# Sparse attention of the last mixers: two PSUM banks in turn in place of three

## The reference

```python
def one_block(args):                       # one block of 128 queries
    dots = jnp.einsum('bqhd,bsd->bqhs', iqb, ik) * idx_scale
    score = jnp.einsum('bqh,bqhs->bqs', iwb * w_scale, jax.nn.relu(dots))
    score = jnp.where(admissible[None], score.astype(jnp.float32), -jnp.inf)
    _, sel = lax.top_k(score, k_sel)       # 256 keys for each query
    ...
    logits = (jnp.einsum('bqhr,bqkr->bqhk', ql, c_sel).astype(jnp.float32) * scale
              + jnp.swapaxes(bias, -1, -2).astype(jnp.float32))
    p = jax.nn.softmax(logits, axis=-1).astype(c.dtype)
    return jnp.einsum('bqhk,bqkr->bqhr', p, c_sel)
```

## Time and profile before

| | before |
|---|---|
| median of three runs | 5201.58 us |
| lowest and highest | 5184.79 and 5215.15 us |
| span of the profiled execution | 5189.6 us |
| TensorE, VectorE, ScalarE busy in the span | 84%, 51%, 37% |
| the thirteen steps that attend tiles 15 to 3 | 3783 to 4945 us of the span |

### The profile page before, as it was taken

One profiled execution on the slowest core, in us unless ns is written; L12 is line 12 of the kernel. 1 busy time (PEld: TensorE's weight loads), 2 busy tenths in 40 slices (PEclk: granted clock), 3 DMA queues, 4 the chain that ended last, 5 costly groups with the idle time before them and its releaser, 6 DMA issues. The chain is left out here.

```text
span 5189.6 us, 65192 instructions
## 1 busy us (share of the span) xinstructions
PE 4361.9 (84%) x23554; PEld 3247.0 (63%) x23554; DVE 2639.9 (51%) x5371; ACT 1922.0 (37%) x3900; POOL 711.8 (14%) x745
## 2 busy tenths in 40 slices
PE   7997999984688888888898999977787878787679
PEld 6885777774566555656787888853344444454467
DVE  3113444445555544444212111138889888888545
ACT  3112323324323333333101101023667776777621
POOL 3102111100000000000000000003222333344400
PEclk9998999985567777778899999976677788778789
DMA  5327666664000000000423212120000000101033
GB/s 184 119 106 239 210 221 204 215 206 139 28 24 24 24 24 24 13 24 3 154 109 115 82 65 81 55 73 17 19 28 29 19 19 19 37 19 35 31 126 118
DMA packets 203393, 425.84 MB, mean 82 GB/s; under 512 B 37224, under 2 KB 67596, under 8 KB 202908
## 3 DMA queue, kind: packets, MB, share of 16 engines
q1 hardware_dynamic: 203072, 421.67, 23.7%
HBM read 299.93 MB, written 121.65 MB: 81 GB/s over the span
## 5 line engine op out<-in xcount | busy, mean ns | idle before, releaser
L3185 POOL TENSOR_TENSOR ds_E<-ds_bT 128x256 f32<-128x256 f32 x112 | 72.8, 650 | 2797.5 <-ACT ds_bT L3154 2620.6
L2718 PE MATMUL ds_big<-ds_ikT,ds_iqT 64*128 64x512 f32 (+3 forms) x608 | 382.0, 759 | 75.4 <-ACT ds_iqT L2695 54.6
L301 PE MATMUL g_acc<-g_ws_hi,g_hT_hi 128*128 128x512 f32 (+1 forms) x1024 | 386.5, 377 | 0.0
L303 PE MATMUL g_acc<-g_ws_hi,g_hT_lo 128*128 128x512 f32 (+1 forms) x1024 | 384.9, 376 | 0.0
L302 PE MATMUL g_acc<-g_ws_lo,g_hT_hi 128*128 128x512 f32 (+1 forms) x1024 | 384.9, 376 | 0.0
L529 PE MATMUL mm_big<-mm_gw_hi,mm_ghT_hi 128*128 128x512 f32 (+1 forms) x768 | 321.4, 418 | 31.0 <-PEq L134 31.0
L2774 DVE TENSOR_SCALAR_CACHE_REDUCE ds_seen<-ds_eq,ds_num 128x2048 uint16<-128x2048 uint16 (+13 forms) x224 | 331.3, 1479 | 26.4 <-issue 4.4
L531 PE MATMUL mm_big<-mm_gw_hi,mm_ghT_lo 128*128 128x512 f32 (+1 forms) x768 | 302.7, 394 | 0.0
L530 PE MATMUL mm_big<-mm_gw_lo,mm_ghT_hi 128*128 128x512 f32 (+1 forms) x768 | 302.0, 393 | 0.0
L2814 ACT ACTIVATE ds_signs<-ds_lo,ds_at 128x2048 bf16<-128x2048 uint16 (+13 forms) x224 | 291.3, 1301 | 1.5
L328 DVE COPY g_stage<-g_acc 128x512 f32<-128x512 f32 (+1 forms) x64 | 41.5, 649 | 459.2 <-PE g_acc L303 459.2
(11 more groups left out here) (519 smaller groups left out, 10155.1 us busy)
## 6 DMA issues: line engine op xcount, KB each, us to landing
mm_ghT_hi<-turned SPq DMA_DIRECT2D x96, 512.0 KB, 3.8
mm_ghT_lo<-turned SPq DMA_DIRECT2D x96, 512.0 KB, 5.5
proj<-g_stage SPq DMA_DIRECT2D x112, 256.0 KB, 2.0
proj<-mm_gstage SPq DMA_DIRECT2D x80, 256.0 KB, 5.0
mm_x<-proj SPq DMA_DIRECT2D x64, 256.0 KB, 3.8
second_raw<-in_w_in SPq DMA_DIRECT2D x56, 256.0 KB, 4.2
proj<-fp_stage SPq DMA_DIRECT2D x48, 256.0 KB, 2.0
mm_graw<-in_w_in SPq DMA_DIRECT2D x40, 256.0 KB, 6.4
```

The source lines that it names most:

```text
L301: pe.matmul(sums, hT.hi[:, k, tile], wt.hi[:, k, 0:width], start=(k == 0), stop=False)
L303: mm = pe.matmul(sums, hT.lo[:, k, tile], wt.hi[:, k, 0:width], start=False, stop=(k == KD - 1))
L2718: pe.matmul(big[:, n % 2, 0:wd], iqT[o, h // 2], b.ikT[o, x:x + wd], start=True, stop=True)\
```

## The change

The list of banks loses its last entry:

```diff
-    turns = in_turn([2, 3, 4], uses)
+    turns = in_turn([2, 3], uses)
```

## The result

| | before | after |
|---|---|---|
| median of four runs | 5204.64 us | 5252.98 us |
| lowest and highest | 5184.79 and 5215.15 us | 5248.38 and 5263.06 us |
| span of the profiled execution | 5189.6 us | 5248.3 us |
| steps that attend tiles 15 to 12 | 458.6 us | 498.8 us |

The kernel is 1.13% slower, ratio 1.0113 with a 95% interval of 1.0094 to 1.0133. Of 5204.64 us that would be 59 us; the two medians lie 48 us apart (0.93%), and the four runs of before scatter by 30 us. The profiled execution took 5250.26 us, of which 5248.3 are the span. So the loss is 48 to 59 us where 30 were forecast.

A forecast was written before the change was run, and what follows sets the result against it. The prediction took VectorE, which hardly ever waits, as the bound, with TensorE close behind. Terms of 20 + 9 + 6 less 5 us absorbed gave 30 us over the median, 5232 us, range 5196 to 5275.

The forecast's parts named there:

- By waits alone the change can only cost: Across the kernel: every old wait is implied by a new one, so nothing starts earlier unless a duration changes.
- term 3: TensorE's clock after longer holds: half of 7 holds at 3.4 us, half reaching VectorE, 6 us; upper bound 24.
- Term 1: L waiting for the previous piece's eviction: 1.0 us at 14 four-piece places, 0.3 at 20 others, 20 us; bounds 0, 53.
- both cases: Head 2 of tiles 14 and 15: the delayed L(2,1) makes L(2,2) late, costing VectorE 1.3 and 1.9 us.
- The worked case of tile 14: Head 2: L(2,1) starts 3.4 us later, work behind it moves 3.5 us, and VectorE loses 1.3 us at L(2,2).
- 34 places: Of some 127 L checked, those that started before the eviction would free one of two banks, 63.8 us together.
- Term 2: T waiting for ScalarE's previous copy in 43 places: 28 us on TensorE, a third counted, 9 us; bounds 0 and 28.
- Clock collapses: Four- and three-piece tiles: long holds send TensorE to 0.50, 24 to 32 episodes, 65 us, 5267 us; chance 0.11.
- if the clock of the steps moves by more than 0.04: Sign that the forecast is wrong, set on TensorE's clock in the steps attending tiles 15 to 3.
- Absorbed: TensorE's idle time in the thirteen steps makes good what is lost: 0 to 12 us, about 5208 us; chance 0.27.
- Every piece serialised: Heads 1 to 3: VectorE waits for each of 120 pieces' matmuls after evicting, 80 to 130 us, 5305 us; chance 0.07.
- Faster: Thirteen steps: TensorE works in denser stretches, its clock falls less often, 28 us less, 5174 us; chance 0.08.

The follow-up runs named there:

- idle holds: Kernel before, three banks; at seven places in tiles 15 to 12 L also waits, TensorE idle, for VectorE's eviction of the piece before: 5230.08 us, ratio 1.0062.
- busy hold: Kernel before, three banks; unread matmuls into L's own bank ahead of L(2,1) in tiles 15 to 12 and L(1,1) in 14 to 12: 5196.38 us, ratio 1.0016.
- e2_rest_only: Against the kernel before: three banks kept for the four-piece tiles, two for all others; 5204.33 us, ratio 1.0031.
- e6_l_later: Changed kernel with each L of heads 1 to 3 placed 0.45 of a piece later in TensorE's list; 5227.48 us, ratio 1.0067 to the kernel before.
- the two with idle holds: Kernel before with L waiting idle for the previous eviction: at seven places 5230.08 us, ratio 1.0062; at only the four L(2,1) 5217.71 us, ratio 1.0049.

## Why the prediction was right or wrong

- **Direction and place: right.** "By waits alone the change can only cost" held, VectorE is what a late logits matmul is lost on, and 40 us stand in the steps of tiles 15 to 12, as said. VectorE's wait for L grew to 62.1 us ("35 us or more"). But these steps grew by 9 to 13 us each, where 3 to 6 were forecast.
- **The step that failed: term 3, with the 6 us for the clock.** It took half of seven long holds to lower the clock, at 3.4 us of TensorE each, and half of that for VectorE. The busy and the idle holds, at seven places, differ in VectorE's wait by 43.7 - 13.1 = 30.6 us, of which 19.2 us are the waits for the four L(2,2). Three errors are in the term. First, the half: the seven were the four L(2,1), and L(3,1) of tiles 11, 9 and 7, and all four L(2,1) lowered the clock; by themselves they make 27.2 of the 34.0 us of the idle holds. Of the other three in the changed kernel the one in tile 7 did (3.85 us), those in tiles 11 and 9 (2.56 and 1.30 us) did not. Second, the price: the low clock comes when TensorE has the two score matmuls, the recurrence's group, a T, a `weigh` and the next L before it, so that 5.3 us of work become 10.2, 4.9 us and not 3.4. Third, halving for VectorE: it has at that place run out of work, and all 4.9 us arrived.
- **Term 1, 20 us for L behind the eviction: too large for what it described.** I worked both cases with full-clock durations. Such a delay without the clock, the busy hold, costs 3.4 us of VectorE's wait over seven of the dearest places, 0.5 us each, where I took 1.0; the whole time says 4 us by the medians and 8 by the ratio. The worked case of tile 14 came to 1.3 us; the busy hold leaves 0.41 us at L(2,1) and nothing at L(2,2). I also counted 34 places late against the eviction; 24 holds are there, 44.9 us, probably since VectorE's later evictions and TensorE's later L move together. The wait was forecast at 40 to 70 us in 35 places.
- **Term 2, 9 us for T behind the copy: small, as taken, and no more.** With two banks for L and one for T the kernel is at +0.12% (-0.01 to +0.24%), so 6 us with an interval from 0 to 12; the upper bound of 28 us is out. The waits moved from `weigh` to T as described.
- **Luck in the sum.** Terms 1 and 2 were put too high for the four-piece tiles and term 3 far too low. The errors offset each other in part, so that 30 us look nearer to the 48 to 59 measured than the mechanism was.
- **The rivals.** "Clock collapses" had the right cause and was given 0.11. It asked for a mean clock of 0.75 or less over the steps; over tiles 15 to 3 it went from 0.79 to 0.78, and over the four steps from 0.80 to 0.76. It was too wide (eight tiles, 24 to 32 episodes) where few episodes sufficed, each dearer than priced. The sign of being wrong, "if the clock of the steps moves by more than 0.04", was set on the wrong stretch: a mean over thirteen steps can't show a few episodes. "Absorbed" is out by 1.0113. "Every piece serialised" is out too: TensorE waits at L in 24 places and VectorE for L in 37, of 120 pieces. "Faster" had the sign of the clock wrong.
- **Small tiles, and a path that has no term.** Tiles 7 to 3 grew by 6.0 us (3.9 in tile 7), where under 1 us each was forecast. By e2_rest_only all tiles of three or fewer pieces cost 0.31% or 16 us, with an interval of 9 to 24, where term 1 had 6 us for its other 20 places. The prediction followed only the late L. In these tiles two thirds of VectorE's added wait is for the relu of the scores, whose matmul stands behind the held L (12.6 us against 6.1 in e2_rest_only), and it goes away in tiles 11 to 8 where L stands behind that matmul (e6_l_later). How far the clock has a part in it was not tested.
- **A point on reading.** The prediction had seen the episode in the profile before: a gap of 2.1 us, then 8 us at 0.57. The other gap there, of 2.2 us without a fall, made me take one half. The same profile shows the gap of 2.6 us ahead of head 1 with 1.2 GHz behind it in tile 14; counting more of such gaps would have been worth the time.

## What to carry to other kernels

Where an engine is to wait in a stream, look what is queued behind the wait: four idle holds of TensorE of 2.6 to 6.1 us cost this kernel not their own length but the doubling of the next 5 us of work, and that was lost whole because another engine had just run dry. Of two interleaved streams through PSUM, give the spare bank to the one whose bank is freed by the engine that bounds (here the logits, 1.1 to 1.3%), not to the one freed by an engine with time (0.1%). A clock raised where no engine is about to wait bought nothing (ratio 0.9999 at 0.839 in place of 0.829). To part the clock's share of a loss from the order's, delay the same work once by idling and once by dead matmuls of the same length.

## What the hardware showed beside this

- Dead matmuls can pay. 24 unread ones, over 21 us of TensorE, made the changed kernel 39 us faster (5250.15 to 5210.8 us on one chip), since they stood in idle holds. Four at the start of each step raised the clock of those 30 us from 0.50 to 0.61 and more, and the time stayed (ratio 0.9999).
- In the steps of tiles 15 to 12 of the changed kernel and of the two with idle holds, all 18 holds of 2.36 to 6.09 us were followed by 1.2 GHz, in 14 of them from the first matmul, in the others within 3 us; at L(1,1), six of the 18, the kernel before had the low clock too in tiles 14 and 12. In the smaller tiles of the changed kernel it was not so each time: a hold of 2.56 us in tile 11 was followed by 2.4 GHz, ones of 1.94 (tile 11), 2.77 (tile 10) and 3.85 us (tile 7) by 1.2. Behind L(2,1) it lasted some 10 us although TensorE was then fully busy (9.99 of 10 us, clock 0.50). Where matmuls filled the hold of L(2,1) it stayed at 2.4 GHz.
- The whole mean of the clock hides this: the profiled execution before has 0.829 over its span, the changed kernel 0.824, the one with idle holds 0.830, more than before, the one with busy holds 0.833.
